# Modulation columns as VectorE multiply-adds behind the pieces of the feed-forwards

## The reference, cut to what matters

```python
c_act = jax.nn.silu(c)                                    # (1, 1024)
for i in range(2):
    mod = (c_act @ mod_w[i] + mod_b[i]).reshape(B, 3, 3, D)   # mod_w[i]: (1024, 9216)
    shift, scale, gate = mod[:, :, 0], mod[:, :, 1], mod[:, :, 2]
    h = rms_norm(x, norm_g[i, 0]) * (1 + scale[:, 0]) + shift[:, 0]
    x = x + 0.5 * gate[:, 0] * swiglu(h, w_gate[i, 0], w_up[i, 0], w_down[i, 0])
    h = rms_norm(x, norm_g[i, 1]) * (1 + scale[:, 1]) + shift[:, 1]
    x = x + gate[:, 1] * attention(h)                     # forgetting attention (i=0), dilated (i=1)
    h = rms_norm(x, norm_g[i, 2]) * (1 + scale[:, 2]) + shift[:, 2]
    x = x + 0.5 * gate[:, 2] * swiglu(h, w_gate[i, 1], w_up[i, 1], w_down[i, 1])
```

## Time and profile before

| | us |
|---|---|
| median of 3 runs | 2281.76 (2279.49 to 2282.95) |
| the profiled execution, its own time | 2281.24 |
| its span, first to last instruction | 2279.9 |
| TensorE busy (matmuls) | 2187.2, 96% |
| VectorE busy | 1365.1, 60% |
| ScalarE busy | 1095.2, 48% |
| mean granted TensorE clock | 0.987 |

### The profile page before, as it was taken

The page is one execution under the profiler, slowest core; times in us unless marked ns, Lnnn a source line. Parts: engine busy times, 40 slices in busy tenths (PEclk is TensorE's granted clock), DMA queues, the critical chain, the costliest instruction groups (busy, mean ns, idle before and its releaser), DMA issues.

```text
span 2279.9 us, 33539 instructions
## 1 busy us (share of the span) xinstructions
PE 2187.2 (96%) x14432; PEld 1894.0 (83%) x14432; DVE 1365.1 (60%) x1776; ACT 1095.2 (48%) x1242; POOL 85.2 (4%) x92
## 2 busy tenths in 40 slices
PE   7999998999999999999899999999999999999998
PEld 5997665898789877678689987898999887998996
DVE  4543666654554466656665455567787664677884
ACT  4443555543444345545544335644555457445552
POOL 1200010000000000000000011000000111000000
PEclk9999999999999999999999999999999999999999
DMA  9776672656657655536265555444655564436551
GB/s 353 264 265 254 223 269 74 234 200 265 218 193 258 258 199 201 211 125 226 75 222 186 187 212 201 146 139 166 203 184 186 169 233 137 169 138 207 182 185 55
DMA packets 274819, 448.64 MB, mean 197 GB/s; under 512 B 10816, under 2 KB 146304, under 8 KB 274416
## 3 DMA queue, kind: packets, MB, share of 16 engines
q1 hardware_dynamic: 270016, 429.07, 54.5%
q0 software_dynamic: 4368, 16.31, 2.0%
q10 hardware_dynamic: 288, 1.11, 0.1%
HBM read 445.40 MB, written 1.06 MB: 196 GB/s over the span
## 4 chain that ended last, share of the span: by engine, by line
PE 78%; ACT 5%; DVE 4%; issue 1%; DMA 0%; POOL 0%; ACTq 0%; SPq 0%; DVEq 0%; POOLq 0%
PE ps L1449 76%; DVE wlo L1875 1%; ACT whi L1670 1%; PE ps L1636 1%; PE ps L1603 1%; ACT S L1670 1%; ACT L1670 1%; ACT xs L1670 0%; PE ps L1593 0%; DMA raw<-in_fox_w_in 0%; ACT xhi L1670 0%; DVE S L2009 0%; DVE x L1911 0%; ACT PT L1670 0%; DVE xs L1904 0%
## 5 line engine op out<-in xcount | busy, mean ns | idle before, releaser
L1875 DVE TENSOR_TENSOR wlo<-raw,whi 128x2048 fp32r<-128x2048 f32 (+1 forms) x339 | 768.2, 2274 | 533.1 <-ACT whi L1670 532.8
L1670 ACT ACTIVATE whi<-raw 128x2048 fp32r<-128x2048 f32 (+1 forms) x339 | 640.8, 1895 | 412.6 <-PE ps L1449 370.9
L1449 PE MATMUL ps<-xhi,whi 128*128 128x256 f32 x2632 | 649.5, 287 | 8.4 <-DVE wlo L1875 3.5
L1449 PE MATMUL ps<-xhi,wlo 128*128 128x256 f32 x2632 | 642.8, 284 | 0.0
L1449 PEld LDWEIGHTS ps<-xhi,whi 128*128 128x128 f32 x2632 | 507.4, 193 | 26.4 <-issue 16.5
L1449 PEld LDWEIGHTS ps<-xhi,wlo 128*128 128x128 f32 x2632 | 507.6, 193 | 1.3 <-issue 1.0
L1449 PE MATMUL ps<-xlo,whi 128*128 128x256 f32 x2632 | 344.3, 283 | 0.1
L1449 PEld LDWEIGHTS ps<-xlo,whi 128*128 128x128 f32 x2632 | 327.6, 192 | 0.5 <-DVE xlo L1975 0.3
L1449 PE MATMUL ps<-whi,xhi 128*128 128x512 f32 x736 | 299.1, 406 | 17.3 <-ACT xhi L1670 11.0
L1449 PE MATMUL ps<-wlo,xhi 128*128 128x512 f32 x736 | 291.9, 397 | 0.0
L1449 PE MATMUL ps<-whi,hhi 128*128 128x512 f32 x528 | 209.5, 397 | 1.9 <-DVE rows L1899 1.0
(11 more groups left out here) (218 smaller groups left out, 1811.9 us busy)
## 6 DMA issues: line engine op xcount, KB each, us to landing
raw<-in_mod_w SPq DMA_DIRECT2D x72, 1024.0 KB, 8.1
raw<-in_w_in SPq DMA_DIRECT2D x52, 1024.0 KB, 4.9
raw<-in_ffn_w_gate SPq DMA_DIRECT2D x88, 512.0 KB, 5.9
raw<-in_ffn_w_up SPq DMA_DIRECT2D x88, 512.0 KB, 6.9
raw<-in_ffn_w_down SPq DMA_DIRECT2D x44, 1024.0 KB, 8.7
raw<-in_w_up SPq DMA_DIRECT2D x88, 512.0 KB, 4.8
raw<-in_dil_w_in SPq DMA_DIRECT2D x36, 1024.0 KB, 5.5
raw<-in_w_down SPq DMA_DIRECT2D x22, 1024.0 KB, 4.9
```

Of the source, the lines that this page charges most:

```text
L1449: return nc.tensor.matmul(o, lhs, rhs, start=start, stop=stop, skip_group_check=True)
L1670: return nc.scalar.activation(o, i, func, **kw)
L1875: V.tensor_tensor(wlo[:, s["c"], 0:s["n"]], raw[:, s["slot"], 0:s["n"]], whi[:, s["c"], 0:s["n"]].bitcast(F32), ALU.subtract).then_inc(sem ...
```

## The change

21 of the 36 modulation units leave `mod_unit`. They are now `mod_half` pairs: a piece of kind "m" for each half, in front of a gate-up step or of every other down step of the four feed-forwards (6, 7, 7 and 1 units). For a half, VectorE runs four steps `mod_acc`: macc = weight rows times the scalar `csil` of that row block, plus macc, of 128x512 each (the first of a unit is a plain multiplication). They are put behind the pieces' matmuls by `run_work`, two for each piece. The slot of the "m" piece is free with the fourth of them (semaphore `mod_acc`). After the eighth, TensorE sums `macc` over the partitions: four matmuls of `macc` against one column of ones for a shift or a scale, or one against all ones for a gate, and this instruction waits for the last `mod_acc`.

The remaining 15 units stay on TensorE: 4 in `start`, 5 in front of the norms, 5 in the forgetting attention (4 before), 1 in the dilated one (5 before). `x_turn` waits for the first half of a tile before its first four transposes and for the second half before the last four. `ftm` and `rtm` are dropped and their uses go to `nbuf` and to the new `mrow`/`macc` pair.

```diff
+    def run_work(self, n=2):
+        for _ in range(min(n, len(self.work))):
+            self.work.pop(0)()
...
@@ feature
             self.used(pc, tok)
+            self.run_work()
             self.run_beside()
...
+    def mod_half(self, i, u, h):
+        pc = self.take()
+        self.used(pc, ("mod_acc", self.acc_named + 4))
+        self.acc_named += 4
+
+        def part(kk):
+            before = self.recent_acc if h or kk else self.acc_free
+            tok = self.recent_acc = self.ev("dve", "mod_acc")
+            self.add("mod_acc", h=h, kk=kk, slot=pc["slot"], landed=pc["landed"], before=before)
+            if h and kk == 3:
+                self.mod_turns.append(lambda: self.mod_turn(i, u, (G3 if self.in_down else D3) - u % 2, tok, True))
+
+        self.work += [lambda kk=kk: part(kk) for kk in range(4)]
...
@@ stage_order
-        fill = {("ffn", 0, 0): [(0, u) for u in (6, 7, 8, 9, 4, 5, 10)], ("mix", 0): [(0, u) for u in range(11, 16)],
-                ("ffn", 0, 1): [(0, 16), (0, 17)] + [(1, u) for u in range(4)],
-                ("ffn", 1, 0): [(1, u) for u in range(4, 10)], ("mix", 1): [(1, u) for u in range(10, 16)],
-                ("ffn", 1, 1): [(1, 16), (1, 17)]}
+        in_norm = {("ffn", 0, 1): (0, 16), ("ffn", 1, 0): (1, 6), ("ffn", 1, 1): (1, 16), ("mix", 0): (0, 10), ("mix", 1): (1, 14)}
+        on_vector = {(0, 0): [(0, u) for u in range(4, 10)], (0, 1): [(0, 17)] + [(1, u) for u in range(6)],
+                     (1, 0): [(1, u) for u in range(7, 14)], (1, 1): [(1, 17)]}
+        fill = {0: [(0, u) for u in range(11, 16)], 1: [(1, 15)]}
...
             for q in range(11):
                 if (i, j, q) not in ((0, 0, 0), (0, 0, 1)):
+                    if q:
+                        half()
                     step("gateup", i=i, j=j, q=q)
-                for m in at[q]:
-                    step("mod", i=m[0], u=m[1])
             for q in range(11):
+                if q in (0, 2, 4, 6):
+                    half()
                 step("down", i=i, j=j, q=q)
...
@@ pe_program, mod_turn and x_turn
+                        if s["acc"]:
+                            ins = mm(ps[:, s["bank"], m:m + 1], macc[:, c], ones[:, 0:1], m == 0, True)
+                        else:
+                            ins = nc.tensor.transpose(ps[:, s["bank"], c], mrow[:, c], ident[:, :])
...
-                    q.wait_ge(s["ready"])
...
                     for m in TURN_ORDER:
+                        q.wait_ge(s["ready"][m // 4])
...
@@ dve_program
+                elif k == "mod_acc":
+                    c = 4 * s["h"] + s["kk"]
+                    w = raw[:, s["slot"], 512 * s["kk"]:512 * s["kk"] + 512]
+                    q.wait_ge(s["landed"])
+                    q.wait_ge(("c_silu", 1))
+                    q.wait_ge(s["before"])
+                    if c:
+                        V.scalar_tensor_tensor(out=macc, in0=w, scalar=csil[:, c, 0:1], in1=macc, op0=ALU.mult,
+                                               op1=ALU.add).then_inc(sem["mod_acc"])
+                    else:
+                        V.tensor_scalar(macc, w, csil[:, 0, 0:1], None, ALU.mult).then_inc(sem["mod_acc"])
```

More of the change, by code:

```diff
@@ L64, in __init__ @@
         self.mod_row_free = None
+        self.acc_free = None
+        self.acc_named = 0
+        self.work = []
+        self.in_down = False
         self.mod_ready = {}
@@ L140, in plan_conv @@
         self.convert_low()
+        while pc["slot_free"] and pc["slot_free"][0] == "mod_acc" and self.count.get("mod_acc", 0) < pc["slot_free"][1]:
+            self.run_work(1)
         c = pc["c"] = self.n_conv % CONV
@@ L272, in mod_turn @@
             tok = self.gate_ready[(i, sub, u % 2)] = self.ev("dve", "mod_col")
-            self.add("gate_spread", g=g, half=u % 2, bank=bank, bank_free=bank_free, mod_row=row, mod_turned=turned,
+            self.add("gate_spread", acc=acc, g=g, half=u % 2, bank=bank, bank_free=bank_free, mod_row=row, mod_turned=turned,
                      rows_in=(f"row_in{g}", self.rows_in[g]))
@@ L276, in mod_turn @@
             return
-        col = self.ev("dve", "mod_col")
-        s = self.add("mod_turn", i=i, u=u, bank=bank, bank_free=bank_free, mod_row=row, mod_turned=turned, mod_col=col,
+        col = None if acc else self.ev("dve", "mod_col")
+        s = self.add("mod_turn", acc=acc, i=i, u=u, bank=bank, bank_free=bank_free, mod_row=row, mod_turned=turned, mod_col=col,
                      shift_read=self.shift_read.get(u // 2))
-        self.free[bank] = col
         tok = s["mod_bias"] = self.ev("dve", "mod_col")
+        self.free[bank] = col or tok
         if kind:
@@ L1008, in step, with half @@
             steps.append(dict(kind=kind, **kw))
-        fill = {("ffn", 0, 0): [(0, u) for u in (6, 7, 8, 9, 4, 5, 10)], ("mix", 0): [(0, u) for u in range(11, 16)],
-                ("ffn", 0, 1): [(0, 16), (0, 17)] + [(1, u) for u in range(4)],
-                ("ffn", 1, 0): [(1, u) for u in range(4, 10)], ("mix", 1): [(1, u) for u in range(10, 16)],
-                ("ffn", 1, 1): [(1, 16), (1, 17)]}
+        in_norm = {("ffn", 0, 1): (0, 16), ("ffn", 1, 0): (1, 6), ("ffn", 1, 1): (1, 16), ("mix", 0): (0, 10), ("mix", 1): (1, 14)}
+        on_vector = {(0, 0): [(0, u) for u in range(4, 10)], (0, 1): [(0, 17)] + [(1, u) for u in range(6)],
+                     (1, 0): [(1, u) for u in range(7, 14)], (1, 1): [(1, 17)]}
+        fill = {0: [(0, u) for u in range(11, 16)], 1: [(1, 15)]}
         def ffn(i, j):
-            fl = list(fill.get(("ffn", i, j), []))
+            halves = [(*m, h) for m in on_vector[i, j] for h in range(2)]
+            def half():
+                if halves:
+                    k, u, h = halves.pop(0)
+                    step("mod_half", i=k, u=u, h=h)
             if (i, j) == (0, 0):
@@ L1043, in mix @@
                             step("fox_f")
-                        for m in fl[:2 if r == 1 else 1] if hh == 0 else ():
+                        for m in fl[:2 if r else 1] if hh == 0 else ():
                             fl.remove(m)
@@ L1299, in build @@
         csil = named("csil", [P, NC, 32])
[L1300 removed]
+        mod_rows = named("mrow", [P, 2, 512])
+        mrow, macc = mod_rows[:, 0, :], mod_rows[:, 1, :]
         rope = named("rope", [P, 2, 2, 16])
@@ L1544, in pe_program @@
                     q.wait_ge(("const_set", 4))
-                    mm(ps[:, s["bank"], :], ones[:, :], mrow[:, :], True, True).then_inc(sem["mod_turned"])
+                    mm(ps[:, s["bank"], :], ones[:, :], macc if s["acc"] else mrow, True, True).then_inc(sem["mod_turned"])
                 elif k == "x_turn":
```

64 lines of the change are left out of this document (35 added, 29 removed).

## The result

The changed kernel takes 2466.0 us (median; 2463.5 to 2468.1), the kernel before 2281.4 (2279.5 to 2283.0): a ratio of 1.081, 95% interval 1.079 to 1.083. The forecast was 2445 with a range of 2385 to 2500. The profiled execution has a span of 2466.3 us.

A forecast was written before the change was run, and what follows sets the result against it. TensorE, busy 96% of the span, was taken to bound the kernel. 2281.2 - 42.6 (products) + 206 (full loops) + 12 (short) - 11 (hidden) - 4 (halves) + 4 (forgetting attention) = 2445.6, forecast 2445 us, range 2385 to 2500.

The forecast's parts named there:

- The loop: Feed-forward steps: refill, weight landing, conversions and multiply-adds chain into 17.5 us against TensorE's 11.5; 34 full rounds, +206 us.
- E: The moment a half's fourth multiply-add ends, at the end of its step, freeing the "m" piece's slot.
- The multiply-add: On VectorE: 0.69 us each, 0.48 for a unit's first; 2.8 us for a half on average.
- The partition sum: On TensorE, per shift or scale: four matmuls with one column, at most the transposes' 0.42 us, which was kept.
- The clock: TensorE after its stops: slower pieces fit in the 6 us per step left free, so nothing was counted.
- the four short ones: Last intervals of the feed-forwards, where the refill is a weight piece: 14.1 or 14.5 us, together +12 us.
- the hidden ones: TensorE's 11 partition sums inside the loops, 0.42 us each; with 6 spreads of 1.03, -11 us.
- forgetting attention: Its extra unit adds two MB to an already full DMA queue: +4 us (0 to 8).
- halves: Transposes by halves: four of eight start 0.44 us earlier in ten norms, -4 us.
- The landing is hidden and the change pays: Rival: weights behind the refill land in time in the feed-forwards; 2234 to 2241 us, 5%.
- The loop is shorter: Rival: landing at 6 us or below and cheaper multiply-adds make steps of 14.5 us; some 2340 us, 8%.
- TensorE's clock: Rival: a lower clock lasts through whole steps, so 23 us of TensorE binds each; some 2630 us, 5%.

The follow-up runs named there:

- the run with the cheaper form: Changed kernel with each multiply-add made a plain multiplication by a scalar; 2427.9 us, ratio 1.064 to the kernel before.
- the kernel without the loop: Changed kernel with the four multiply-adds of a half put ahead of the step's two conversions in VectorE's order; 2251.9 us, ratio 0.987.
- the kernels with the other order: Two edits of the changed kernel: SyncE issues "m" pieces behind the next two weight pieces, 2276.4 us; VectorE's multiply-adds ahead of the conversions, 2251.9 us.
- the best kernel: Changed kernel with multiply-adds ahead of conversions, plus a 22nd unit on VectorE in (0,0), leaving forgetting attention four; 2244.7 us, ratio 0.983.

## Why the prediction was right, and which of its terms were off

**The mechanism** is as predicted, in every link. The gated product recurs 34.9 us after the last but one (90.13, 125.06), 17.5 for a step, though the two products between these are 14.5 and 20.5 apart; the copies wait for the DMAs of gate and up (6.94 + 1.00 us in the step shown; 6 were forecast), SyncE's queue waits for the multiply-adds, and the next "m" piece is issued 0.03 us after the fourth. From the first to the last gated product, (0,1) and (1,0) grew by 51 and 49 us (125.3 to 176.7, 126.4 to 175.2); "about 60" was forecast, though nine loops by 6 are 54 and four products leave, which is 46. The second block changed by -0.7. The queue's order alone takes 190 us away, seven eighths of the bytes 65.

**The loop.** Forecast 17.5, measured 17.54 in the step shown, and 17.7 in the mean. Term by term in that step: landing 8.2 after E (8.3), ScalarE 1.95 (1.92), two conversions 4.4 (4.42), multiply-adds 1.45 and 1.53, together 3.0 (2.8). 34 full loops are 602 us where 595 had been worked out, that is +7. The loops over gate-up steps of (0,1) hold most of it: 17.1 to 20.1. In the burst of 527.20 the last DMA of A has 0.96 us to its issue and this landing:

```profile
raw<-in_ffn_w_up SPq DMA_DIRECT2D x1, 512.0 KB, 8.5
```

It is 9.5 us after the first issue, inside the bounds 7.2 to 9.8, while the "m" piece in front of it lands in 5.2 as at 104.71. Why the same burst takes 1.3 us longer there was not found. The Trainium skill, "DMA: Bandwidth & Descriptors", section on the anatomy of one DMA, was cited with an estimate of 6.8 us for 2 MB in one DMA of another issuing path. The bursts measured 8.2 and 9.5 after the first issue, so here the trace doesn't agree, and the loops of 16.0 us and the 2390 that followed from it were wrong.

**The multiply-add.** 0.69 was taken from the addition of two tensors. It lasts 0.749, and the four of the step shown 2.98:

```profile
L1949 DVE SCALAR_TENSOR_TENSOR mrow<-raw,csil,mrow 128x512 f32<-128x512 f32 x147 | 110.2, 749 | 3.0
```

It is dearer than the nearest row, with 693, and by the run with the cheaper form every microsecond of it counts.

**The partition sum** was the wrong bound. "The transposes have the same four weight loads and 128 columns, so they bound it from above by 0.42" is false. The page shows it as x104 for 13 units, eight to a unit and not four. In the kernel without the loop the group of eight takes 0.95 and costs 0.87, where the transposes took 0.60 and cost 0.42. Its weight loads take 202 ns there, those of the transposes 141. A form that the trace of before doesn't hold had been bounded from above by one that only looked alike. It is the +5.9 above; in the changed kernel 11 of the 13 sums hide behind the loop.

**The clock** was the term put at nothing, and it is the largest single part of the miss. "The loop leaves TensorE 6 us per step, so I count nothing" holds inside the loops. It doesn't hold behind the last stop of a feed-forward: no loop follows there, TensorE has its weights and works without a gap, and at first at the lower clock. TensorE at that sum in (0,0), and windows from the last sum or spread of (0,0), (0,1) and (1,0) on (us, busy, then granted clock, DMA share, GB/s):

```profile
259.20 1.83 PE L1489 MATMUL ps<-ones,mrow 128*128 128x1 f32 x8 [6.24 <-DVE mrow L1949]
```

```profile
259.20:266.90 7.70, 7.70 (x23) 6.39 (x24) 2.52 (x3) 0.00 (x0) 0.00 (x0) 0.51 0.89 320
718.70:724.60 5.90, 5.83 (x13) 3.98 (x14) 2.89 (x2) 0.00 (x0) 0.00 (x0) 0.54 0.84 283
998.00:1004.60 6.60, 6.52 (x21) 5.55 (x22) 2.36 (x2) 0.00 (x0) 0.00 (x0) 0.55 0.83 294
```

From this sum or spread to the product of the next norm it takes 32.5, 20.3 and 20.6 us. The same pieces take 29.0, 17.8 and 17.8 by the kernel with the multiply-adds ahead (its own stretches there, less one down piece of 5.6 that it has more). That is 3.5 + 2.6 + 2.8, about 9 us. In (1,1), behind a wait of 3.42 us, the granted clock is 0.66 over 8.1 us, an estimated 3 more.

**The rest.** The miss is 20 us (2466.0 less 2445.6). The terms that have a measured size: full loops +7; the four short ones +1; sums +5.9, of which the hidden ones give back 3.7 (they and the hidden spreads, at a cost of 0.87 and 0.85, are 14.7 and not 11); forgetting attention 1 to 3; halves 1.5; the clock 9 to 12. Together 22 to 27, so something else in the kernel got cheaper by a few us, as in the kernel with the multiply-adds ahead, and that stays open. Forgetting attention was given 4 beside its product and came to 5.1 there and 7 here, inside the bounds of 0 and 8. That the time came out within 1% is in part luck, since terms of several us missed in both directions. (Two slips without weight: the dilated attention loses four units and not five, the 21 are right; and by the terms named for it the range is 2377 to 2496, not 2385 to 2500.)

**The rivals.** "The landing is hidden and the change pays" is what the kernels with the other order do (2276, 2252); the condition named for it, that A's DMA doesn't stand behind the refill, is the very edit of the first. In the changed kernel it does, and it didn't happen. "The loop is shorter", at 14.5, is ruled out even at 128 KB to a piece, where it is 15.6. "TensorE's clock", in the form that a step of 23 us binds in place of the loop, is ruled out too. Windows of after, over (0,0), (0,1), and (1,1), which has two halves only (us, busy, then granted clock, DMA share, GB/s):

```profile
85.00:235.00 150.00, 114.73 (x768) 108.35 (x769) 72.33 (x73) 39.77 (x33) 0.45 (x1) 0.83 0.55 186
489.00:636.00 147.00, 108.68 (x811) 106.92 (x811) 69.41 (x70) 40.59 (x33) 0.00 (x0) 0.85 0.53 172
1345.00:1500.00 155.00, 150.80 (x1100) 142.83 (x1099) 80.36 (x59) 62.27 (x48) 0.00 (x0) 0.98 0.60 195
```

The granted clock is 0.83 to 0.85, so about a third of these stretches at 1.2 GHz, after stops such as the one of 8.43 us ahead of the spread at 122.36; that spread takes 2.05 us, twice the 1.03 that it takes at 2.4 GHz. TensorE's stops at the sums are 7.8 us in the mean (155.6 in 20) and not 11, since the slower matmuls fill a part of the room. The Trainium skill, "TensorE: Matmul & The Clock Gate", on the return of the clock under sustained work, agrees: the stretch with one short stop has 0.98. "By that rule 2445 stays" was too low by the 9 to 12 us behind the last stops. No run tried the clock by itself. When the loop goes, the clock comes back by itself (2209 us of TensorE become 2145 in the best kernel).

## What to carry to other kernels

When an operation moves to another engine, look at which instruction frees its buffer now, and at what stands behind the refill of that buffer in the DMA queue. A load that is late for nobody can hold back loads whose own buffers have been free for long, and if their data stands ahead of the freeing instruction in program order, the prefetch has become a loop whose length is a sum over several engines and a landing, whatever their busy shares are (60% and 44% for the two engines here). Two edits open it, each one enough here: issue the refill behind the loads that are needed sooner, or free the buffer at the beginning of the step and not at its end. And when an engine is said to have room, look at the end of the stretch as well, where it has none.

## What the runs showed of the hardware that had not been expected

- A 128x512 multiply-add in fp32 (a tensor by a per-partition scalar, plus a tensor) takes 0.749 us on VectorE, more than the plain operation of two tensors (0.693) and 1.55 times the scalar multiplication (0.483).
- An fp32 sum over partitions with 128x128 weights and one column is two passes to a matmul in the records. Four such take 0.95 us and cost 0.87, where four transposes of 128 columns took 0.60 and cost 0.42: fewer columns made it no cheaper.
- After a wait of 4.7 to 6.2 us with nothing else on TensorE, the granted clock was 0.51 to 0.55 over the next 6 to 8 us, while TensorE worked without a stop; this cost 2.6 to 3.5 us each time.
- In a burst of 1 MB and 2 x 512 KB into an idle queue, leaving out half of the first piece shortened the loop of (0,0) by 1.0 us, and leaving out seven eighths by 1.9. With only 128 KB in front, the 1 MB behind it still landed 6.4 us after the first issue, of which 1.0 is the issuing of two DMAs ahead of the last.
